# A two-block transformer kernel on one core: woven projections of the second attention, parameters packed on the host, and one 512-column matmul in place of two of 256 in the expert loops

## The reference

```python
# second attention of the first model (MLA)
proj = h @ w_in                                   # 1024 -> 384 + 256 + 32
c_q  = rms_norm(proj[..., :384], q_norm_g)
c_kv = rms_norm(proj[..., 384:640], kv_norm_g)
k_pe = apply_rope(proj[..., 640:], cos, sin)
q    = (c_q @ w_uq).reshape(b, s, 16, 64 + 32)    # its last 32 are turned by apply_rope
kv   = (c_kv @ w_ukv).reshape(b, s, 16, 64 + 64)
# PEER, twice: 16384 experts, 8 heads x 16 chosen for each token
h = einsum("cd,ced->ce", x, u[chosen]);  a = g * gelu(h);  out = einsum("ce,ced->cd", a, v[chosen])
```

## Time and profile before

| | us |
|---|---|
| median of 3 runs | 2785.22 (2783.14 to 2787.93) |
| profiled execution | 2784.15 |
| its span, first to last instruction | 2782.3 |
| PE busy | 2582.9 (93%) |
| DVE busy | 1797.5 (65%) |
| ACT busy | 1299.3 (47%) |
| POOL busy | 784.6 (28%) |

### The profile page before, as it was taken

One profiled execution on the slowest core, in us unless ns is written; L12 is line 12 of the kernel. 1 busy time (PEld: TensorE's weight loads), 2 busy tenths in 40 slices (PEclk: granted clock), 3 DMA queues, 4 the chain that ended last, 5 costly groups with the idle time before them and its releaser, 6 DMA issues.

```text
span 2782.3 us, 47349 instructions
## 1 busy us (share of the span) xinstructions
PE 2582.9 (93%) x15959; PEld 2317.0 (83%) x15959; DVE 1797.5 (65%) x3387; ACT 1299.3 (47%) x1919; POOL 784.6 (28%) x786
## 2 busy tenths in 40 slices
PE   7879987899899888999999999889888999999998
PEld 5679865798789787899999998669787899999997
DVE  5768755687557998455555555567997555555555
ACT  4656545565444165444444444454165444444443
POOL 0300003000000101355555555230101355555554
PEclk9999999999999999999999999989999999999999
DMA  5135641356554413666666665424413666666664
GB/s 187 53 122 182 191 125 46 114 182 189 159 167 136 136 39 106 185 187 187 183 188 187 183 188 180 121 76 132 126 39 121 184 188 186 184 187 186 184 188 143
DMA packets 170078, 420.43 MB, mean 151 GB/s; under 512 B 13968, under 2 KB 66637, under 8 KB 169726
## 3 DMA queue, kind: packets, MB, share of 16 engines
q1 hardware_dynamic: 162894, 412.82, 48.4%
q10 hardware_dynamic: 7088, 6.33, 0.8%
HBM read 418.02 MB, written 1.08 MB: 151 GB/s over the span
## 4 chain that ended last, share of the span: by engine, by line
PE 77%; DVE 15%; ACT 3%; issue 3%; DVEq 1%; POOL 1%; SPq 0%; ACTq 0%; DMA 0%; POOLq 0%
PE PS L447 24%; PE PS L449 24%; PE PS L448 24%; DVE oh L1887 3%; DVE oh L1884 1%; DVE lo L1337 1%; DVE arena L1850 1%; PE PS L602 1%; DVE arena L1854 1%; DVEq L1887 1%; DVE arena L1784 1%; DVE arena L1788 1%; DVE arena L1785 1%; ACT arena L976 1%; DVE arena L1472 0%
## 5 line engine op out<-in xcount | busy, mean ns | idle before, releaser
L1337 DVE TENSOR_TENSOR lo<-raw,hi 128x1024 fp32r<-128x1024 f32 x732 | 1007.6, 1381 | 777.3 <-ACT hi L908 775.1
L908 ACT ACTIVATE hi<-raw 128x1024 fp32r<-128x1024 f32 x732 | 765.8, 1055 | 502.1 <-PE PS L449 483.9
L447 PE MATMUL PS<-xh,hi 128*128 128x256 f32 x2784 | 791.7, 284 | 2.6 <-DVE xl L1385 2.6
L448 PE MATMUL PS<-xl,hi 128*128 128x256 f32 x2784 | 791.5, 284 | 0.0
L449 PE MATMUL PS<-xh,lo 128*128 128x256 f32 x2784 | 791.3, 284 | 0.0
L447 PEld LDWEIGHTS PS<-xh,hi 128*128 128x128 f32 x2784 | 536.4, 193 | 12.9 <-issue 4.1
L448 PEld LDWEIGHTS PS<-xl,hi 128*128 128x128 f32 x2784 | 536.6, 193 | 8.0
L449 PEld LDWEIGHTS PS<-xh,lo 128*128 128x128 f32 x2784 | 536.3, 193 | 0.0
L447 PE MATMUL PS<-hi,Ah 128*128 128x512 f32 x1024 | 403.9, 394 | 10.8 <-DVE lo L1337 7.1
L449 PE MATMUL PS<-hi,Al 128*128 128x512 f32 x1024 | 404.7, 395 | 0.0
L448 PE MATMUL PS<-lo,Ah 128*128 128x512 f32 x1024 | 404.1, 395 | 0.0
(11 more groups left out here) (224 smaller groups left out, 2968.3 us busy)
## 6 DMA issues: line engine op xcount, KB each, us to landing
raw<-in_peer_u SPq DMA_DIRECT2D x256, 512.0 KB, 3.6
raw<-in_peer_v SPq DMA_DIRECT2D x256, 512.0 KB, 4.3
raw<-in_ffn_w_up SPq DMA_DIRECT2D x88, 512.0 KB, 3.6
raw<-in_ffn_w_down SPq DMA_DIRECT2D x44, 512.0 KB, 3.8
raw<-in_peer_w_q SPq DMA_DIRECT2D x32, 512.0 KB, 4.7
raw<-in_da_w_qkv SPq DMA_DIRECT2D x24, 512.0 KB, 4.0
raw<-in_conv_w_in SPq DMA_DIRECT2D x24, 512.0 KB, 3.6
raw<-in_attn_w_qkv SPq DMA_DIRECT2D x12, 512.0 KB, 4.2
```

The lines of the kernel that those rows point to most:

```text
L447: pe.matmul(o, ah, bh, start=start, stop=False)
L448: pe.matmul(o, ah, bl, start=False, stop=False)
L908: cp.activation(hi[:, s, 0:size], raw[:, s, 0:size], ACT.Copy).then_inc(hi_made, 1)
L1337: V.tensor_tensor(lo[:, s, 0:size], raw[:, s, 0:size], hi[:, s, 0:size].bitcast(F32), ALU.subtract).then_inc(lo_made, 1)
```

## The change

Three independent edits. The diff, cut to what matters (`first` only shifts the column index in `turned`):

```diff
@@ PEER loop: PE @@ xx holds xh and xl side by side: xx = sb("xx", [P, 2, KD, T]); xh, xl = xx[:, 0], xx[:, 1]
                     if i >= LEAD + 2:
-                        pe.wait_ge(gelu_made, h0 + i - 1 + exa)
+                        pe.wait_ge(h_summed, h0 + i - 1 + exa)
...
-                        m = mm3(PS[:, 6 + i % 2, 0:T], hi[:, s, w], lo[:, s, w], xh[:, k, :], xl[:, k, :],
-                                k == 0, k == KD - 1)
+                        both = PS[:, 6 + i % 2, :].rearrange("p (c t) -> p c t", c=2)
+                        pe.matmul(both, hi[:, s, w], xx[:, :, k, :], start=k == 0, stop=False)
+                        m = pe.matmul(both[:, 0, :], lo[:, s, w], xh[:, k, :], start=False, stop=k == KD - 1)
@@ PEER loop: ACT @@
-                    act.wait_ge(split_used, u_block(layer, i) + 1 + 2 * exa)
-                    act.wait_ge(S("a_made"), a0 + i - 1 + exa)
-                    cp.activation(gl[:, i % 2, :], PS[:, 6 + i % 2, 0:T], ACT.Gelu).then_inc(S("gelu_made"), 1)
+                    act.wait_ge(S("h_summed"), (P - LEAD) * layer + i - LEAD + 1 + exa)
+                    cp.activation(gl[:, i % 2, :], gl[:, i % 2, :], ACT.Gelu).then_inc(S("gelu_made"), 1)
@@ PEER loop: DVE @@
-                with dve.Fori(0, left // 4, 1) as it:
-                    for p in range(p0, p0 + 4):
-                        split(M + p, BLK, it * 4)
+                def add_parts(i, ex=0):
+                    dve.wait_ge(split_used, u_block(layer, i) + 1 + 2 * ex)
+                    dve.wait_ge(S("a_made"), P * layer + i - 1 + ex)
+                    V.tensor_reduce(gl[:, i % 2, :], PS[:, 6 + i % 2, :].rearrange("p (c t) -> p t c", c=2), AX.X,
+                                    ALU.add).then_inc(S("h_summed"), 1)
...
+                with dve.Fori(0, (P - LEAD - 2) // 2, 1) as it:
+                    for x in range(2):
+                        add_parts(LEAD + x, it * 2)
+                        split(M + p0 + 2 * x, BLK, it * 4)
+                        split(M + p0 + 2 * x + 1, BLK, it * 4)
@@ MLA: PE @@
-            pe.wait_ge(S("mla_c_made"), 4)
-            turn("mc", lambda t, k: proj[:, t, k * P:(k + 1) * P])
-            pe.wait_ge(xt_lo, xt["mc"][0] + 5)
-            rows_linear("mla_uq", [([2, 1], 512, 0)] * 3)
+            def turn_kv():
+                pe.wait_ge(S("mla_c_made"), 4)
+                turn("mck", lambda t, k: proj[:, t, MLA_QR + k * P:MLA_QR + (k + 1) * P])
+            pe.wait_ge(S("mla_c_made"), 2)
+            turn("mcq", lambda t, k: proj[:, t, k * P:(k + 1) * P])
+            pe.wait_ge(xt_lo, xt["mcq"][0] + 3)
+            rows_linear("mla_uq", [([2, 1], 512, 0)] * 3, {0: turn_kv})
+            pe.wait_ge(xt_lo, xt["mck"][0] + 2)
@@ MLA: ACT (DVE likewise, with scaled_part) @@
+            def q_part():
+                squares(0, 0, MLA_QR)
+                splits_to(plan["mla_uq"][0] + 1)
             rows_linear("mla_in", [([2] * 4, 512, 0), ([4, 4], 160, 0)],
-                        lambda t, g: proj[:, t, 0:512] if g == 0 else proj[:, t, 512:672])
+                        lambda t, g: proj[:, t, 0:512] if g == 0 else proj[:, t, 512:672], {0: q_part})
+            turned("mcq", G_MQ)
+            splits_to(plan["mla_uq"][0] + 2)
+            squares(1, MLA_QR, MLA_QR + MLA_KR)
@@ MLA: DVE, behind the copies of the mla_ukv groups 0 and 1 instead of behind all four @@
+                if g < TT:
+                    rope_q(g)
@@ start: ACT issues seven loads, SP five DMAs before the weights @@
+            load(con[:, P:], consts[:, P:])
+            load(lamv, laid_rows[:, 0:4 * DA_DH].rearrange("o (k d) -> o k d", d=DA_DH).to_broadcast([P, 4, DA_DH]))
...
             norm("n0")
-            act.wait_ge(S("params_turned"), 1)
+            splits_to(1)
+            act.wait_ge(S("columns_in"), 16)
...
-            sp.dma_start(X[:, :, :], I["x"][0].rearrange("(t p) d -> p t d", p=P)).then_inc(S("x_in"), 16)
+            for t in range(TT):
+                sp.dma_start(X[:, t, :], I["x"][0][t * P:(t + 1) * P, :]).then_inc(S(f"x_in{t}"), 16)
+                if t == 0:
+                    sp.dma_start(con[:, 0:P], consts[:, 0:P]).then_inc(S("ident_in"), 16)
+            sp.dma_start(pT[:, :], laid_columns).then_inc(S("columns_in"), 16)
```

More of the change, by code:

```diff
@@ L104, with program @@
 KEPT = LEAD - 2
-def program(nc, I, consts, hot, out):
+def program(nc, I, consts, hot, laid_columns, laid_rows, out):
     plan = {}
@@ L819, in _ @@
                 rows_group(B + 4 * g, G0 + g, [2] * 4, 512)
+            pe.wait_ge(params_in, 16 * N_PARAMS)
+            b = aux("rel", [(S("rel_table"), 1)])
+            pe.matmul(PS[0:GQA_H, b, :], relv[0:BUCKETS + 1, :], hotv[0:BUCKETS + 1, :],
+                      start=True, stop=True).then_inc(aux_full, 1)
             with pe.Fori(0, 2, 1) as it:
@@ L916, in splits_to, with turned @@
                     nxt[0] += 1
-            def turned(name, gain):
+            def turned(name, gain, first=0):
                 base, kcs = xt[name]
@@ L942, in norm @@
                 whole = name not in ("f0", "f1")
-                if adds:
-                    cp.activation(small[:, 58:59], ss[:, 4:5], ACT.Sqrt)
+                if not adds:
+                    act.wait_ge(S("set_up"), 1)
+                cp.activation(small[:, 58:59], ss[:, 4:5], ACT.Sqrt)
                 for q, (t, w) in enumerate(quarters):
@@ L1145, in _, with squares @@
-            act.wait_ge(S("mla_ms"), 2)
-            cp.activation(sst[:, 4:8], sst[:, 0:4], ACT.Sqrt).then_inc(S("mla_rt"), 1)
+                    if g in after:
+                        after[g]()
+            copies = tcopies["mla_in"]
+            def squares(x, c0, c1):
+                act.wait_ge(S("copied_dve"), copies + x + 1)
+                act.wait_ge(S("copied_act"), copies + x + 1)
+                for t in range(TT):
+                    cp.activation(XS[:, t, c0:c1], proj[:, t, c0:c1], ACT.Square,
+                                  accum_out=sst[:, 2 * x + t:2 * x + t + 1]).then_inc(S("mla_sq"), 1)
+                act.wait_ge(S("mla_ms"), x + 1)
+                cp.activation(sst[:, 4 + 2 * x:6 + 2 * x], sst[:, 2 * x:2 * x + 2], ACT.Sqrt).then_inc(S("mla_rt"), 1)
@@ L2190 @@
     for name in _INS:
+        if name in _COLUMNS or name in _ROWS:
+            continue
         a = np.asarray(inputs[name])
@@ L2198 @@
         I[name] = nc.dram_tensor("in_" + name, a.shape, mybir.dt.from_np(a.dtype), kind="ExternalInput").ap()
+    columns = [np.asarray(inputs[name]).reshape(-1, P) for name in _COLUMNS[:-2]]
+    for l in range(2):
+        columns += [np.asarray(inputs[name])[l].reshape(-1, P) for name in _COLUMNS[-2:]]
+    rows = [np.asarray(inputs[name]).reshape(1, -1) for name in _ROWS]
+    laid = []
+    for name, a in (("laid_columns", np.concatenate(columns).T), ("laid_rows", np.concatenate(rows, axis=1))):
+        arrays[name] = np.ascontiguousarray(a)
+        laid.append(nc.dram_tensor(name, a.shape, F32, kind="ExternalInput").ap())
     packed, hot = shape_constants()
```

177 lines of the change are left out of this document (79 added, 98 removed).

## The result

The changed kernel takes 2758.56 us (median of 4 runs, 2757.24 to 2763.68), the kernel before 2784.62 (4 runs, 2783.14 to 2787.93): ratio 0.9908, 95% interval 0.9891 to 0.9925. It is 26 us faster, where 28 us slower was forecast. The time is that of rival A (2758); the sign of the forecast was wrong. The profiled execution has a span of 2755.5 us against 2782.3, so 26.8 are to be found.

The account below looks back on a forecast made before the run. PE, busy 93% of the span, was taken as the bound. 2785.2 - 5.8 (start) - 7.6 (second attention) - 13.7 (merged products) + 55 (stalls) = 2813 us; range over all 2752 to 2825, likeliest case 2800 to 2825.

Parts of the forecast that it names:

- rival A: PEER loop: POOL gets in, `Al` ends by 4.9 every time, PE never stalls; 2758 us, chance 0.26.
- the sign of the forecast: Whole kernel: slower, 2813 us from a median of 2785.2; chance of slower 0.64.
- What bounds it: PEER loop: nothing but PE's own stream sets the time, 5.64 us a pair, 204 pairs.
- the u products, PE's side: `hidden` in the loop: two 256-column matmuls become one of 512, 2.81 us against 2.87, 13.7 us less in all.
- The 4.1 us: `hidden` in the loop: alternative gain from the skill's 2.5 ns saved per merged pair, instead of 13.7 us.
- The u products, the other side: PEER loop: the DVE sum delays everything behind gelu by 0.74 us, so `Al` comes late and PE stalls.
- Where DVE has its next operation ready, POOL gets nothing: Rule for the loop from one lead-stage row: `Al` waits through both DVE splits and ends at 6.03 us.
- the stall of 0.54 us in every second pair: PE before `values` in the loop: 0.46 us waiting plus 0.08 for a slower first matmul; chance 0.57.
- the gap of 0.63 us between the splits: DVE in the loop: idle time in which `Al` runs before the change, claimed to vanish with the delay.
- a turn at a delay of the gelu of about 0.71 us: PEER loop: the gelu delay at which the outcome turns between no PE stall and a stall.
- Start: Before the first attention: earlier scaling and splits, bias-table matmul and DMA issue off PE's path; net -5.8 us, bounds -3 and -9.
- MLA: Second attention's projections: query scaling under the second group, ropes between copies; -7.6 us, bounds -4 and -10.

Follow-up runs that it names:

- the part alone: Kernel before with only the u products changed (512-column matmuls, sum on DVE, gelu from SBUF): 2771.66 us, ratio 0.9957.
- the merging taken back: Changed kernel with each 512-column u product done as two matmuls of 256, all else kept: 2771.17 us, ratio 0.9944.
- two more reductions: Changed kernel with two extra unused DVE reductions ahead of the sum in each pair of the loop: 2985.05 us.
- four pieces: Changed kernel with DVE's split of the u block in the loop done as four operations of 256 elements, ready together: 2785.74 us.
- four fillers: Changed kernel with four unused DVE products of 256 elements right behind the sum of each pair: 2813.62 us.
- DVE held: Changed kernel with DVE waiting in the lead stage, before the product behind the split under way, until POOL's third `Al` is done: 2755.59 us.
- both splits ready: Changed kernel with DVE also waiting for the v block's high part before it splits the u block: 2799.34 us.
- fillers behind POOL's product: Changed kernel with four unused DVE products behind each pair's sum, held until POOL has done its first product of the pair: 3010.53 us.
- more reductions, splits ready: Changed kernel with two extra DVE reductions a pair, and DVE waiting for the v block's high part before the u block's split: 3038.07 us.
- part alone, by the medians: Kernel before with only the start changed (packed parameters, x in two halves, parameter loads on ACT's queue): 2780.63 us, ratio 0.9982.
- the run in which the waits are gone: Changed kernel with DVE's fourth first split ahead of the lambda chain and key clearing behind the second group's splits: 2752.93 us, ratio 0.9893.
- 4.5 either way alone: Kernel before with only the second attention's woven projections: 2772.11 us, ratio 0.9960.

## Why the prediction was wrong

*What bounds it*, *the u products, PE's side*: right. 2.81 us was forecast for `hidden`, and 2.81 is there; 13.7 us was forecast, and 12.4 (the part alone) and 12.6 (the merging taken back) were measured by the medians; the two loops of the profile gain 12.1, or 0.060 us a pair for 0.067. The 4.1 us estimated from the Trainium skill's formula ("TensorE: Matmul & The Clock Gate", Back-to-back issue gap) is excluded by the loops and by the interval of the part alone (7 to 16 us).

*The u products, the other side*: this failed, and in one step: "Where DVE has its next operation ready, POOL gets nothing". With it failed the stall of 0.54 us in every second pair, 55 us of the sum; PE is never idle in the 400 us of the loop. Up to it, every time of the loop is right within 0.03 us: the reduction 0.69, the gelu 0.73 later, both splits back to back. Then `Al` is served behind the split under way, in 1.60 us, and PE has its operand 0.78 us early. The runs put in its place: in the loop POOL waits for at most one operation of DVE, with the next one ready for 0.8 us (two more reductions), with four pieces or four fillers in a row, in a loop or written out. I had one case of the contrary, and it is real (3.13 us fall to 1.35 with DVE held), but it is one in each lead stage, and I made a rule of it for 204 pairs. The Trainium skill ("SBUF — State Buffer", Who interferes with whom) says that the two exclude one another, which the stretched times here agree with (`Al` 1.60 us for 0.74, a split 1.75 to 1.80 for 1.23); it doesn't say what I had taken for the rule, that a ready DVE keeps POOL out.

The row that spoke for the other reading was there too: in the earlier trace rows the u-split meets `Ah`, waits, and `Al` behind it waits and is served, orderly. I argued there that the gap of 0.63 us between the splits was what let `Al` in. The gap went, and `Al` is as fast.

*Rival A* had the time, and gave two reasons for it. The first, a faster reduction with a turn at a delay of the gelu of about 0.71 us, is wrong: with the gelu 1.3 us later still, `Al` takes 1.59 us. The second, that POOL is served first when both wait, is what the runs show.

*What neither had is DVE's round.* The reduction hangs on DVE's queue, behind the splits: reduction, gelu, ACT's high part, u-split, v-split, next reduction. From the rows of the changed kernel: 1285.53 - 1283.40 = 2.13 to the first split, 3.47 for both, 5.60 less the overlap at the end. The changed kernel's reductions of 1200 to 1600 us (busy us, mean ns, then the idle time ahead of them):

```profile
L1969 DVE TENSOR_REDUCE gl<-PS 128x256 f32<-128x512 f32 x72 | 49.8, 692 | 0.0
```

With the merging taken back they come every 5.647 us, PE's pair, and the 71 of this stretch have 3.1 us of idle time ahead of them: DVE waits some 0.04 us for each product. In the changed kernel they come every 5.587 us with no idle time ahead of any, while PE has no gap either: the two rounds are equally long within some 0.01 us. Every kernel that adds to DVE's round pays all of it, 204 times:

| kernel | a reduction every, us | (that - 5.587) x 204 | measured above 2758.6 |
|---|---|---|---|
| split in four pieces | 5.728 | 29 | 27 |
| both splits ready | 5.794 | 42 | 41 |
| four fillers | 5.853 | 54 | 55 |
| two more reductions | 6.700 | 227 | 226 |
| fillers behind POOL's product | 6.841 | 256 | 252 |
| more reductions, splits ready | 6.966 | 281 | 279 |

(first to last reduction in 1200 to 1600 us.) The agreement of the columns says only that the added time is all in the loop. That DVE's round sets it is said by its queue: in none of the six is there idle time ahead of the first reduction of a pair. So the change fits with nothing to spare: by this table 0.1 us more in any step of that round would have cost 20 us, more than its u products gain.

*Start*: the mechanism was right, PE starting 8.6 us sooner and meeting the same DVE chain, waits of 3.67 us for 4 to 5; the size was -3.3 (profile) and -3.4 (part alone, by the medians) for -5.8, inside its bounds. Of the 2.5 us short, 1.0 was short at 32.21 already, 6.1 us earlier where DVE's gain was put at 7.1. The rest is behind it, and there the missing term is PE's clock: it drops behind the wait, where I had set it full. That is shown by the run in which the waits are gone and the clock stays at 1.0.

*MLA*: -7.6 forecast, -8.7 in the profile, -12 with some 4.5 either way alone, all of it outside the loops. The steps were near: -6.9 for the first matmul of `mla_uq` (measured -7.2 from the group-0 copy), 1.09 us left of the 5.68, and 1.31 + 1.22 back behind the ropes where I had 3.2. The forecast had no term for the clock, which rose in this stage from 0.83 to 0.89; how much of the 8.7 that is was not measured.

*The sum.* Rival A's 2758 meets 2758.6 in part by luck. By what the profile gives to the edit the sum is 2785.2 - 10.8 - 12.1 + 1.6 = 2763.9: the start and the second attention before the loops, the two loops, and what is lost ahead of them. The 5.5 us between the loops, which no term of the forecast has, make up the rest; a difference of that size is also within the interval of the ratio.

## What to carry to other kernels

A row that shows one engine shut out by another is one event; before it becomes a rule for a loop, look in that loop for the times the two already meet and how they were served there. Before a new operation is put on an engine that is "half busy", add up its round, what each of its operations waits for included, and set that against the bound engine's: DVE was 54% busy before, and one reduction of 0.69 us made its round as long as PE's. And an idle stretch of PE near the start cost more than its length, since the clock fell behind it (5.0 us for 3.67 us of waits): work that only DVE needs later (clearing, constants) belongs behind the operations that PE waits for.

## What the runs showed of the hardware

- DVE and POOL on SBUF operands take turns by operation: four DVE operations of 256 elements, with one of POOL's between the third and the fourth, stretch to 1.97 us from some 1.4 (three starts 0.33 apart and 0.41), and POOL's products take 0.88 and 0.92 instead of 0.74. Once in each lead stage POOL instead stood through four DVE operations, 3.12 to 3.35 us. It is not POOL's loop and not DVE's; what it is was not found.
- A DVE reduction over two fp32 elements of PSUM that lie 1 KB apart runs at the copy's price, 0.69 us for 512.
- At the full granted clock one matmul of 512 columns takes 0.231 us where two of 256 take 0.240, also if its columns come in two runs 8 KB apart; over the loops eight such mergings save 0.060 us.
- Between executions of like kernels the granted clock of the stretch from 400 to 760 us differs (0.92 before, 0.93 after, 0.96 in the changed kernel's second profile), and the span with it: 2755.5 and 2751.7 us for the same program. At the first `Al` of the lead stage the second of these is 5.8 us ahead (1064.77 for 1070.56). Differences of a few us between two single profiles are therefore read from waits, or from stages at one clock, and not from spans.
